# First block of a two-block network: one stream of dense products with the steps of three mixers woven in, x normed first

## The chip, the cores and the metric

The kernel runs on one core of a Trainium2 chip. The metric is device time of one execution in microseconds (us). The engines of the core are TensorE (PE in the rows; PEld is its weight load), VectorE (DVE), ScalarE (ACT), GpSimd (POOL) and SyncE (SP), which issues the DMAs.

## The reference

512 tokens of width 1024 go through a first block and then a second. All data is float32. The change is in the first block:

```
hn = rmsnorm(x, norm_g);  z = hn @ w_in          # aq ak av ag | mq mk mv mo mi mf mg | gq gk gv ga gg
y_a = band_chunk_attention(aq, ak, av, rel_bias) * silu(ag)              # 6 heads of 64
qk  = silu(causal_conv([mq, mk], conv_w))                                 # 4 taps
y_b = sigmoid(mo) * head_rmsnorm(mlstm_chunkwise(qk, mv, mi, mf)) * silu(mg)   # 6 heads of 64
y_c = head_rmsnorm(gla_chunkwise(gq, gk, gv, logsigmoid(ga @ w_alpha + b_alpha) / 16)) * silu(gg)   # 4 heads
x   = rmsnorm(x + [y_a, y_b, y_c] @ w_out, final_g)
```

The second block has a memory of 256 tokens (`mem_2`), whose keys and values (`memk`, `memv`) are made by two dense products; two layers (attention with forget gates, then multi-head latent attention, each with cross attention to the memory) and a convolutional feed-forward after each. It is not touched, except that `memk` and `memv` are computed at another time.

## The kernel before

**Engines and steps.** `schedule()` (line 2384) is one list of step names. Each engine's program runs through the whole list and, at each name, resumes its own generator for this stage (`pe_att`, `act_att`, `dve_att`, ...). So the order of work on every engine is the order of the list, and each engine's queue is in order. Semaphores tie the engines together: `q.wait_ge(*K.at(name))` waits for the event `name`. A name `barN` makes ScalarE, VectorE and GpSimd wait for all engines; it stands where memory is handed from one stage to the next.

**Stages of the first block**, in this order: `mem` (norm and products of the memory, then the norm of x and its transposes), `proj1` (dense: aq, ak, ag, av), `att`, `ya` (attention times silu(ag)), `proj2` (dense: gates, mo, mqk with convolution, mg, mv), `ml` (mLSTM, one head a step), `proj3` (dense: gg, gqk, gv, and six transposes), `gla` (gated linear attention), then `wo1` (output projection, residual, norm).

**Dense products** are float32 by three products of a high and a low part (`mm3`, lines 286 to 288). The weights come in chunks of at most 128 x 1536. A chunk n goes into the staging tile n mod 3 (DMA, line 251), ScalarE copies it to `whi` (line 269), VectorE makes `wlo` (line 278); all three have three buffers. `due` says at which step an engine splits chunk n. `pe_fm` makes a product with channels on partitions, 24 products of 512 columns; `pe_pair` makes two at a time; `pe_tm` makes one with tokens on partitions, four token tiles, in two phases with one chunk each. The results go to PSUM banks, seven of them in the ring `RA`, and are evacuated by `act_hi` (line 366 or 368) and `dve_lo` (375, 377), or `act_evac` (408) and `dve_evac` (413).

**Attention** handles items (head, tile of 128 queries), two heads at a time. At step t: scores of two items in three passes (lines 689, 692, 695), bias and maximum on VectorE (797, 800), exponential on ScalarE (762), transposes of item t-3 (710), evacuation on ScalarE (408), product with v of item t-5 (724).

**mLSTM**: per head, A (1051), scores (1058), decay on ScalarE (1083), its triangle on GpSimd (1155), product of both on VectorE (1112), output (1069); then denominators and a norm per head, `hm` scaled (1138) and multiplied by the gate into `yt` (1142).

**Gated linear attention**: levels 8, 9, 10 (tile to tile), then 0 to 6 (within a tile, by halving), then 7 (diagonal). For levels 0 to 6: a difference of `bT` on VectorE (1277), absolute value and exponential on ScalarE (1302, 1304), times k on VectorE (1279) and times q on GpSimd (1319), 16 products on 32 rows each (1339), four masked copies into `ATT` on VectorE (1394). At the end the outputs (1351, 1354).

Of the kernel before, what the change touches and what calls it, by code (L numbers as in the profile page):

```python
# [13 lines left out]
F32 = mybir.dt.float32  # L14
# [7 lines left out]
P = 128  # L22
# [113 lines left out]
class Ring:  # L136
# [10 lines left out]

    def take(self, q, name):
# [79 lines left out]


# [68 lines left out]
def pe_fm(e, q, K, key, x, kt, n, ring=None, rows=P, name=None):  # L298
# [7 lines left out]
    z.then_inc(*K.pe.up(name or key, ("wused", i)))  # L306


def pe_pair(e, q, K, keys, x, kt, n, ring=None):
# [3 lines left out]
    for k in range(kt):  # L313
        for key, (i, hi, lo), o in zip(keys, two, outs):
# [5 lines left out]
            if k == kt - 1:  # L320
                z.then_inc(*K.pe.up(key, ("wused", i)))


def pe_tm(e, q, K, key, g, x, tiles, cols, mid=None):
# [11 lines left out]
    z.then_inc(*K.pe.up(("wused", i)))  # L336
# [4 lines left out]
    for c in range(tiles):  # L341
# [5 lines left out]
        z.then_inc(*K.pe.up((key, g, "c", c), *[("wused", i)] * (c == tiles - 1)))  # L347
# [111 lines left out]
def sp_init(e, q, K):  # L459
    mem = K.d["mem_2"].rearrange("a (c p) n -> p (a c) n", p=P)  # L460
    x = K.d["x"].rearrange("a (c p) n -> p (a c) n", p=P)
    for c in range(2):
        e.dma_start(K.memt[:, c, :], mem[:, c, :]).then_inc(*K.mem_in[c].up(("mem_in", c), by=16))
    e.dma_start(K.vc[:], K.d["vecs"]).then_inc(*K.consts_in.up(by=16))
    e.dma_start(K.fb[:], K.d["fox_b_f_2"].rearrange("a n -> n a")).then_inc(*K.consts_in.up("consts", by=16))
    for _ in range(3):
        sp_load(e, q, K)
    for c in range(4):
        e.dma_start(K.xt[:, c, :], x[:, c, :]).then_inc(*K.x_in[c].up(("x_in", c), by=16))
# [6 lines left out]
def act_mem(e, q, K):  # L476
    q.wait_ge(*K.at("epsc"))
# [4 lines left out]
    q.wait_ge(*K.at("consts"))  # L482
    for kt in range(8):
        act_hi(e, q, K, ("m", "hi", kt), ("memT", kt), K.mh[:, kt, :], K.col("mem_norm", kt))
    yield
    act_token_squares(e, q, K, "x", K.xt, 4, 0, "x_in")
    q.wait_ge(*K.at(("x", "sum")))
    act_rstd(e, q, K, "x_r", K.small[:, 16:20], K.small[:, 16:20], D)
    for m in range(2):
        t = K.tmp.take(q, ("mksq", m))  # L490
        q.wait_ge(*K.at(("memk", m)))
        e.activation(t[:, 0:256], K.bank(("memk", m))[:, 0:256], ACT.Square).then_inc(*K.act.up(("mk", "sq", m)))
    yield
    for m in range(2):
        t = K.tmp.take(q, ("mkr", m))
        q.wait_ge(*K.at(("mksum", m)))
        act_rstd(e, q, K, ("mkr", m, "made"), t[:, 0:256], K.bank(("mksum", m))[:, 0:256], 64, frees=[("mksum", m)])
    yield
    act_evac(e, q, K, ("vmem", 0), ("memv", 0, "c", 0), K.vmem[:, 0, :], K.bank(("memv", 0, "c", 0))[:, 0:256])
    yield  # L500
    yield
# [5 lines left out]
def dve_mem(e, q, K):  # L507
# [5 lines left out]
    yield  # L513
    for kt in range(8):
        dve_lo(e, q, K, ("m", "lo", kt), ("memT", kt), ("m", "hi", kt), K.ml[:, kt, :], K.mh[:, kt, :],
               K.col("mem_norm", kt))
    yield
    dve_token_sums(e, q, K, "x", 4, 0)
    q.wait_ge(*K.at("x_r"))
    for c in range(4):  # L520
        e.tensor_scalar(K.yt[:, c, :], K.xt[:, c, :], K.small[:, 16 + c:17 + c], None, MUL).then_inc(*K.dve.up(("yt", c)))
    yield
    for m in range(2):
# [78 lines left out]
def dve_proj1(e, q, K):  # L602
# [7 lines left out]
    for _ in range(6):  # L610
        yield
# [2112 lines left out]
```

## Time and profile before

| | us |
|---|---|
| median of 3 runs | 1734.3 (1734.26 to 1743.34) |
| profiled execution, its time | 1752.93 |
| profiled execution, span | 1751.2 |
| mean granted TensorE clock | 0.939 of 2.4 GHz |
| end of the first block up to its output projection | 409.5 us of the span |

The page lists the busy time of each engine and, for 40 equal slices of the span (43.8 us each), the busy share in tenths and TensorE's granted clock in tenths of full speed (9 is 0.9 or more). The chain that ended last goes back from the last instruction, each piece to what released it; it shows what each moment waited for. A float32 product of the mixers has two records, so x8 in the chain is four products.

### The profile page before, as it was taken

Reading aid. Unit: us, or ns where it says so; the run is one execution under the profiler, and the core shown is the slowest. Engines: PE = TensorE matmul, PEld = TensorE weight load, DVE = VectorE, ACT = ScalarE, POOL = GpSimd, SP = SyncE. Lnnn points to the kernel's source line nnn. Section 1 sums busy time; section 2 is a strip of 40 time slices with the busy share of each in tenths; the row PEclk is TensorE's granted clock in tenths of the full one; section 3 lists DMA queues with packets and bytes.
Section 4 is the critical chain, followed back from the end, with each engine's and each line's share of the span. In section 5 each row is a group of like instructions: output and inputs, shape, how many; then the busy total and the mean of one; then the engine's idle time right before and its main releaser. Section 6 shows DMA issues by size and latency. Waiting matters only on the chain.

```text
span 1751.2 us, 20800 instructions
## 1 busy us (share of the span) xinstructions
PE 1647.5 (94%) x8398; PEld 1367.0 (78%) x8398; DVE 829.5 (47%) x1308; ACT 696.8 (40%) x1242; POOL 358.2 (20%) x285
## 2 busy tenths in 40 slices
PE   6999999949899999989999999988899899999999
PEld 6988887839678877868888888656788688888887
DVE  5332625563343466365433443337774544334442
ACT  6343432422456343344422443335553444324431
POOL 0000021320034100133401442103301244104420
PEclk9968985957899999999999999999999999999999
DMA  5401210201123100222322332111001233323331
GB/s 197 150 24 42 96 49 0 100 1 49 36 74 114 65 1 1 84 72 96 115 90 85 96 110 95 40 51 43 25 1 61 69 100 105 112 72 97 101 122 42
DMA packets 36736, 126.36 MB, mean 72 GB/s; under 512 B 4112, under 2 KB 8864, under 8 KB 36640
## 3 DMA queue, kind: packets, MB, share of 16 engines
q1 hardware_dynamic: 36640, 125.03, 22.2%
q8 instruction: 66, 1.08, 0.3%
q14 instruction: 30, 0.25, 0.0%
HBM read 122.92 MB, written 2.10 MB: 71 GB/s over the span
## 4 chain that ended last, share of the span: by engine, by line
PE 83%; DVE 8%; ACT 6%; issue 2%; DMA 1%; POOL 0%; SPq 0%; ACTq 0%; DVEq 0%
PE bank L286 22%; PE bank L287 22%; PE bank L288 22%; PE bank L724 4%; PE bank L710 2%; PE bank L1069 2%; PE bank L1058 1%; ACT tmp L762 1%; DVE tmp L1579 1%; PE bank L689 1%; DVE hlo L1583 1%; PE bank L1339 1%; ACT hhi L1571 1%; PE bank L355 1%; PE bank L1556 1%
## 5 line engine op out<-in xcount | busy, mean ns | idle before, releaser
L286 PE MATMUL bank<-hhi,whi 128*128 128x512 f32 (+1 forms) x1040 | 408.4, 393 | 3.6 <-DVE wlo L278 3.6
L287 PE MATMUL bank<-hlo,whi 128*128 128x512 f32 (+1 forms) x1040 | 406.1, 391 | 0.0
L288 PE MATMUL bank<-hhi,wlo 128*128 128x512 f32 (+1 forms) x1040 | 405.9, 390 | 0.0
L278 DVE TENSOR_TENSOR wlo<-wstage,whi 128x1024 fp32r<-128x1024 f32 (+3 forms) x206 | 279.6, 1359 | 224.9 <-ACT whi L269 218.2
L269 ACT CAST whi<-wstage 128x1024 fp32r<-128x1024 f32 (+3 forms) x206 | 229.4, 1115 | 174.3 <-PE bank L288 148.8
L1899 DVE SCALAR_TENSOR_TENSOR cr<-bank,vc,cr 128x511 f32<-128x511 f32 (+1 forms) x176 | 131.7, 749 | 225.6 <-ACT cr L1842 222.5
L286 PEld LDWEIGHTS bank<-hhi,whi 128*128 128x128 f32 (+1 forms) x1040 | 194.7, 187 | 47.8 <-DVE wlo L278 5.5
L287 PEld LDWEIGHTS bank<-hlo,whi 128*128 128x128 f32 (+1 forms) x1040 | 194.7, 187 | 42.8 <-issue 1.6
L288 PEld LDWEIGHTS bank<-hhi,wlo 128*128 128x128 f32 (+1 forms) x1040 | 194.6, 187 | 42.9 <-issue 0.8
L1842 ACT ACTIVATE cr<-bank,vc 128x512 f32<-128x512 f32 x88 | 68.5, 781 | 257.3 <-PE bank L288 254.1
L1941 POOL TENSOR_TENSOR cr<-cr,cr 128x512 f32<-128x512 f32 x44 | 91.6, 2082 | 283.3 <-DVE cr L1899 260.6
L286 PE MATMUL bank<-ahi,whi 128*128 128x512 f32 x352 | 139.5, 396 | 0.0
L288 PE MATMUL bank<-ahi,wlo 128*128 128x512 f32 x352 | 139.1, 395 | 0.0
L287 PE MATMUL bank<-alo,whi 128*128 128x512 f32 x352 | 139.0, 395 | 0.0
L286 PE MATMUL bank<-whi,hhi 128*128 128x384 f32 (+1 forms) x400 | 131.0, 328 | 0.0
L287 PE MATMUL bank<-wlo,hhi 128*128 128x384 f32 (+1 forms) x400 | 129.8, 325 | 0.0
L288 PE MATMUL bank<-whi,hlo 128*128 128x384 f32 (+1 forms) x400 | 129.6, 324 | 0.0
L1947 POOL TENSOR_TENSOR alo<-cr,ahi 128x512 fp32r<-128x512 f32 x44 | 96.8, 2201 | 120.5 <-ACT ahi L1854 120.5
L710 PE MATMUL bank<-ident,tmp 128*128 128x128 f32 x364 | 74.9, 306 | 14.3 <-ACT tmp L762 6.8
L1923 DVE TENSOR_TENSOR xT<-bank,xT 128x512 f32<-128x512 f32 x32 | 22.1, 692 | 127.4 <-PE bank L288 127.4
L286 PEld LDWEIGHTS bank<-whi,hhi 128*128 128x128 f32 x400 | 77.6, 194 | 1.6 <-issue 0.8
L288 PEld LDWEIGHTS bank<-ahi,wlo 128*128 128x128 f32 x352 | 66.0, 187 | 16.0
(358 smaller groups left out, 2390.5 us busy)
## 6 DMA issues: line engine op xcount, KB each, us to landing
wstage<-in_wts SPq DMA_DIRECT2D x148, 512.0 KB, 3.5
wstage<-in_wts SPq DMA_DIRECT2D x32, 704.0 KB, 4.0
wstage<-in_wts SPq DMA_DIRECT2D x18, 768.0 KB, 4.4
xt<-in_x SPq DMA_DIRECT2D x4, 512.0 KB, 9.3
out<-ob SPq DMA_DIRECT2D x8, 256.0 KB, 2.3
U<-in_rel_ext SPq DMA_DIRECT2D x6, 256.0 KB
wstage<-in_wts SPq DMA_DIRECT2D x3, 384.0 KB, 2.9
memt<-in_mem SPq DMA_DIRECT2D x2, 512.0 KB, 4.0
```

What stands on the lines that cost most here:

```text
L269: e.copy(K.whi[i % 3][:, 0:w], K.stage[i % 3][:, 0:w]).then_inc(*K.act.up(("whi", i)))
L278: e.tensor_tensor(K.wlo[i % 3][:, 0:w], K.stage[i % 3][:, 0:w], K.whi[i % 3][:, 0:w].bitcast(F32), SUB).then_inc(*K.dve.up(("wlo", i)))
L286: e.matmul(o, lh, rh, start=start, stop=False)
L287: e.matmul(o, lh, rl, start=False, stop=False)
L288: return e.matmul(o, ll, rh, start=False, stop=stop)
L710: z = e.transpose(b[:, j * P:(j + 1) * P], K.tmp[A.name, "P", t][:, j * P:(j + 1) * P], K.ident[:])
L724: z = e.matmul(o, A.pt[A.name, "pt", t][:, j * P:(j + 1) * P], A.heads[h].v(j), start=j == 0, stop=j == n // P - 1)
L1069: z = e.matmul(b[:, i * 65:(i + 1) * 65], scm[:, o:o + P], K.mva[:, J, h, :], start=J == 0, stop=J == i)
L1842: e.activation(t[:], K.bank(key)[:], ACT.Identity, scale=K.col(f"cw{l}", 3 * ch + 2), bias=K.col(f"cb{l}", ch)).then_inc(*K.act.up((key, " ...
L1899: e.scalar_tensor_tensor(out=t[:, s:T], in0=b[:, 0:T - s], scalar=K.col(f"cw{l}", 3 * ch + 2 - s), in1=t[:, s:T], op0=MUL, op1=ADD).then_i ...
L1941: e.tensor_tensor(g[:], g[:], v[:], MUL).then_inc(*K.pool.up(("gated", l, ch), frees=[((up, 22 + ch), "cr")]))
L1947: e.tensor_tensor(alo[:, ct, :], g[:], ahi[:, ct, :].bitcast(F32), SUB).then_inc(*K.pool.up(("alo", l, hv, ct), frees=[((up, 11 * hv + ct) ...
```

## The change

- The `mem`, `proj1`, `proj2`, `proj3` stages become one, `den`, of 48 steps. `x` (two steps) goes ahead of it: x is loaded first, normed tile by tile, transposed, split. The memory's products are steps in `den`.
- `weave` mixes steps: 34 of attention with 22 of `den` (av to mqk), 17 of mLSTM with 11 (mo to gv), 16 of gated linear attention with 11 (gv, gg, ag). The barriers `bar0` to `bar3` are gone; instead, single waits (`("att", "fin", 2)`, `("ml", "y", 5)`) guard memory that is used again.
- Banks: mixers have banks 0 to 5, dense products a ring of two (`RP`, banks 6 and 7). Attention has three banks for scores instead of four, two for transposes, one for outputs instead of two. `pe_tiles` replaces `pe_tm` in the block: one bank per token tile, both weight chunks held through all four tiles.
- A chunk is split at the first step after the last use of chunk n-3.
- SiLU and sigmoid are made of exp, ln, exp; the SiLU table isn't loaded in the block any more. For the mLSTM gate, sigmoid(mo) and silu(mg) are joined in logarithms.
- mLSTM has 20 steps (two heads and one tile column at a time) instead of 9; its gate is one multiply per head.
- Levels 0 to 6 of gated linear attention: the difference moves from VectorE to GpSimd.
- `ya` moves from VectorE to GpSimd, to the end, after `ag`.
- x is read from memory a second time for the residual (`again`), as its first tile is overwritten.
- Small tensors move within SBUF, and the scratch for descriptors is made smaller.

```diff
 def schedule():
-    out = ["init"] + ["mem"] * 7 + ["bar0"] + ["proj1"] * 15 + ["att"] * 34 + ["ya", "bar1"]
-    out += ["proj2"] * 23 + ["ml"] * 9 + ["bar2"] + ["proj3"] * 13 + ["gla"] * 16 + ["bar3"]
+    out = ["init"] + ["x"] * 2 + ["den"] * 3
+    out += weave(("att", 34), ("den", 22)) + weave(("ml", 17), ("den", 11)) + ["ml", "masks", "ml", "ml", "again", "masks"]
+    out += weave(("gla", 16), ("den", 11)) + ["den"]
     out += ["wo1"] * 23 + ["norm0", "bar4"] + ["fox"] * 25 + ["foxatt"] * 74
+def weave(*parts):
+    at = [((i + 0.5) / n, k, name) for k, (name, n) in enumerate(parts) for i in range(n)]
+    return [name for _, _, name in sorted(at)]

@@ due
-    return K.first_step[max(n - 2, 0)] - (n < 2) <= g
+    if n < 3:
+        return K.first_step[0] - (n < 2) <= g
+    return K.last_step[n - 3] < g

+def pe_tiles(e, q, K, key, g, x, tiles, cols, extra=None):
+    two = [K.chunk(q, key, g, half) for half in range(2)]
+    for c in range(tiles):
+        b = K.RP.take(q, (key, g, "c", c))
+        for k in range(8):
+            i, hi, lo = two[k // 4]
...
+            z = mm3(e, b[:, 0:cols], x.hi[:, k, c * P:(c + 1) * P], x.lo[:, k, c * P:(c + 1) * P],
+                    hi[:, k % 4, :], lo[:, k % 4, :], k == 0, k == 7)
...
+        yield

+def pe_den(e, q, K):
...
+    pe_pair(e, q, K, [("aq", 0), ("ak", 0)], x, 8, T, K.RP)
+    yield from pe_tiles(e, q, K, "av", 0, x, 4, 384)
...
+    for kt in range(6):
+        q.wait_ge(*K.at(("ya", 3) if kt < 3 else ("ml", "y", 5)))
+        pe_turn(e, q, K, ("yT", kt), lambda c: K.yt[:, c, kt * P:(kt + 1) * P], 4)

@@ act_den, mg
+        act_sigmoid_ln(e, q, K, ("mg", c), t[:, 0:384], K.bank(("mg", 0, "c", c))[:, 0:384], ("mg", 0, "c", c))
+        q.wait_ge(*K.at(("mg", "both", c)))
+        e.activation(t[:, 0:384], t[:, 0:384], ACT.Exp, scale=-1.0).then_inc(*K.act.up(("mg", "sig", c)))

@@ pool_level
     if li < 7:
+        s = 64 >> li
+        t = K.ltp.take(q, ("gl", "t", li))
...
+        e.tensor_tensor(tv, bv, bv[:, :, s - 1:s].to_broadcast([P, T // (2 * s), 2 * s]), SUB).then_inc(*K.pool.up(("gl", "d", li)))
+        q2 = K.qlp.take(q, ("gl", "q", li))
         q.wait_ge(*K.at(("gl", "e", li)))
...
+        e.tensor_tensor(q2[:], K.gq[:], t[:], MUL).then_inc(*K.pool.up(("gl", "qd", li), frees=[("gl", "t", li)]))

@@ act_gla and dve_gla, levels 8 to 10
+            q.wait_ge(*K.at(("ml", "y", 5)))
```

The order of `pe_den` is: aq 0 with ak 0; av; aq 1; ak 1; the memory's transposes (`memT`); memk 0, memk 1; memv; gate; aq 2 with the rows `frow` and `alrow`; ak 2; mv; six mqk; mo; gqk 0; mg; gqk 1; gv; gg; ag; six transposes `yT`. A product with tokens on partitions takes one step for each tile.

## Rows read from the trace of the kernel before

**Rows 1.** The page: granted clock of TensorE in 40 slices.

```profile
PEclk9968985957899999999999999999999999999999
```

**Rows 2.** Windows: length; PE, PEld, DVE, ACT, POOL busy (count); clock; DMA; GB/s.

```profile
0.00:35.00 35.00, 21.40 (x149) 20.54 (x150) 18.66 (x31) 24.14 (x56) 2.52 (x15) 0.95 0.62 232
35.00:101.00 66.00, 66.00 (x337) 60.15 (x336) 21.78 (x22) 22.05 (x28) 0.41 (x1) 1.00 0.38 123
101.00:150.00 49.00, 47.38 (x255) 41.54 (x255) 17.82 (x84) 22.85 (x72) 0.00 (x0) 0.58 0.00 1
150.00:244.00 94.00, 91.73 (x469) 80.65 (x468) 42.06 (x49) 36.30 (x48) 10.33 (x9) 1.00 0.27 87
244.00:305.00 61.00, 61.00 (x180) 41.90 (x178) 26.67 (x54) 15.11 (x41) 9.98 (x28) 0.53 0.00 1
305.00:345.00 40.00, 39.49 (x274) 37.06 (x273) 22.47 (x34) 18.39 (x32) 15.94 (x29) 0.94 0.32 109
345.00:410.00 65.00, 36.81 (x358) 33.52 (x355) 37.66 (x68) 13.85 (x31) 12.44 (x7) 0.52 0.00 1
...
600.00:700.00 100.00, 93.31 (x786) 77.90 (x784) 65.42 (x175) 41.57 (x136) 0.00 (x0) 1.00 0.02 7
```

**Rows 3.** The chain, dense products: start us, length us, what.

```profile
13.12 0.36 PE bank L316
...
35.03 0.34 PE bank L316
...
98.16 0.17 PE bank L287
...
310.18 0.12 PE bank L286
```

**Rows 4.** The chain, same positions in attention pairs and in mLSTM heads.

```profile
105.99 0.72 PE bank L689 x2
...
140.64 0.72 PE bank L689 x2
...
279.01 2.00 PE bank L1051 x2
...
290.03 2.00 PE bank L1051 x2
```

**Rows 5.** The chain in gated linear attention and the start of the output projection.

```profile
354.79 2.19 PE bank L1339 x32
...
358.39 0.64 ACT lt L1304
...
360.64 2.18 PE bank L1339 x32
...
392.25 1.47 PE bank L1351 x6
...
409.51 0.43 PE bank L286
```

**Rows 6.** Groups of instructions, 0 to 42 us: squares of x.

```profile
L394 ACT ACTIVATE tmp<-xt 128x512 f32<-128x512 f32 x8 | 4.9, 616 | 0.0
...
L394 ACT ACTIVATION_READ_ACCUMULATOR tmp<-xt 128x1 f32 x8 | 1.5, 187 | 0.0
```

**Rows 7.** Groups, 38 to 102 us: the splits of a chunk of 1536.

```profile
L278 DVE TENSOR_TENSOR wlo<-wstage,whi 128x1536 fp32r<-128x1536 f32 x5 | 8.8, 1759 | 16.6 <-ACT whi L269 16.6
L269 ACT CAST whi<-wstage 128x1536 fp32r<-128x1536 f32 x5 | 7.4, 1482 | 11.3 <-PE bank L288 11.3
```

**Rows 8.** Instructions on the tile hm: ns min/median/max, first and last start.

```profile
L1138 DVE TENSOR_TENSOR hm<-hm,small x6: 420/896/903, 281.9 to 312.7; 128x256 f32<-128x256 f32 x6
```

**Rows 9.** Groups, 345 to 410 us: the level loop.

```profile
L1394 DVE COPY_PREDICATED ATT<-msk,bank 128x512 f32<-128x512 int32 x28 | 17.8, 714 | 1.2 <-PE bank L1339 1.2
...
L1319 POOL TENSOR_TENSOR ql<-gq,lt 128x512 f32<-128x512 f32 x7 | 12.4, 1777 | 41.5 <-ACT lt L1304 41.5
...
L1279 DVE TENSOR_TENSOR kl<-gk,lt 128x512 f32<-128x512 f32 x7 | 4.8, 692 | 9.5 <-ACT lt L1304 9.5
```

More of the change, by code:

```diff
@@ L227, in chunk, with used @@
         return i, hi, lo
+    def used(self, i):
+        if self.counting:
+            self.last_step[i] = self.step
+        return "wused", i
 def half(h):
@@ L492, in act_mem @@
         e.activation(t[:, 0:256], K.bank(("memk", m))[:, 0:256], ACT.Square).then_inc(*K.act.up(("mk", "sq", m)))
+        yield
+    act_evac(e, q, K, ("vmem", 0), ("memv", 0, "c", 0), K.vmem[:, 0, :], K.bank(("memv", 0, "c", 0))[:, 0:256])
+    mk_norm(0)
     yield
[L494 to L497, printed above, removed]
+    mk_norm(1)
@@ new lines, in act_den @@
+    for i in range(6):
+        conv(MQK[i])
+        if i:
+            conv_silu(MQK[i - 1])
+        yield
+    for c in range(4):
+        b = ("mo", 0, "c", c)
+        q.wait_ge(*K.at(("memv", 0, "c", 1)))
+        q.wait_ge(*K.at(b))
+        e.activation(K.G[:, c, :], K.bank(b)[:, 0:384], ACT.Exp, scale=-1.0).then_inc(*K.act.up(("mo", "exp", c), frees=[b]))
+        q.wait_ge(*K.at(("mo", "exp", c)))
+        e.activation(K.G[:, c, :], K.G[:, c, :], ACT.Ln, bias=1.0).then_inc(*K.act.up(("mo", "ln", c)))
+        if c == 0:
+            conv_silu(MQK[5])
+        yield
@@ new lines, in act_den @@
+    q.wait_ge(*K.at(("att", "fin", 2)))
+    q.wait_ge(*K.at(("gqk", 0)))
+    e.activation(K.gq[:], K.bank(("gqk", 0))[:], ACT.Identity, scale=32 ** -0.5).then_inc(*K.act.up("gq", frees=[("gqk", 0)]))
+    yield
+    for c in range(4):
+        t = K.tmp.take(q, ("mg", c))
+        act_sigmoid_ln(e, q, K, ("mg", c), t[:, 0:384], K.bank(("mg", 0, "c", c))[:, 0:384], ("mg", 0, "c", c))
+        q.wait_ge(*K.at(("mg", "both", c)))
+        e.activation(t[:, 0:384], t[:, 0:384], ACT.Exp, scale=-1.0).then_inc(*K.act.up(("mg", "sig", c)))
+        yield
@@ L566, in pe_proj1 @@
[L566 to L582 removed]
+    akk(2)
@@ L683, in score @@
     def score(ts):
-        at = [(t, A.items[t][1], A.heads[A.items[t][0]], A.n(t), K.RS.take(q, (A.name, "S", t))) for t in ts]
+        at = [(t, A.items[t][1], A.heads[A.items[t][0]], A.n(t), A.S.take(q, (A.name, "S", t))) for t in ts]
         z = {}
@@ L1328, in pe_gla @@
             k2, q2 = K.kl["gl", "k", li], K.ql["gl", "q", li]
-        banks = [K.RA.take(q, ("gl", "B", li, h)) for h in range(4)]
+        banks = [K.RG.take(q, ("gl", "B", li, h)) for h in range(4)]
         rows = [slice(32 * h, 32 * h + 32) for h in range(4)]
@@ L2402, with run @@
 SCHEDULE = schedule()
-def run(e, q, K, signal, stages, ahead=None):
+def run(e, q, K, signal, stages, ahead=None, behind=None):
     begun = {}
@@ L2514, in pairs, with above @@
         return Ring(K, [Buffer(K, tuple(sb(f"{name}{p}{i}", shape, F32R, scope) for p in "hl"), after) for i in range(n)])
+    @contextmanager
+    def above(n):
+        with ExitStack() as scope:
+            if n:
+                sb(f"below{next(count)}", [P, n // 4], scope=scope)
+            yield scope
+    count = itertools.count()
     banks = [Buffer(K, ctx.enter_context(nc.psum_tensor(f"bank{i}", [P, 512], F32))) for i in range(8)]
@@ L2566, in memory @@
-    with ExitStack() as s:
-        K.fgr = sb("fgr", [P, D], scope=s)
-    first.close()
+    with above(35328) as s:
+        K.dts, K.scs, K.hm = ring("dt", 3, [P, T], s), ring("scm", 4, [P, 1280], s), sb("hm", [P, 4, 6, 64], scope=s)
+        K.kl, K.ql, K.lt = ring("kl", 2, [P, T], s), ring("ql", 2, [P, T], s), ring("lt", 2, [P, T], s)
+        K.qlp, K.ltp = (Ring(K, r.buffers[::-1], r.place) for r in (K.ql, K.lt))
+        K.gq, K.gk, K.gv = sb("gq", [P, T], scope=s), sb("gk", [P, T], scope=s), sb("gv", [P, 4, 256], scope=s)
+        K.msk = sb("msk", [P, 7, P], scope=s)
```

1027 lines of the change are left out of this document (531 added, 496 removed).

## The prediction

> **What bounds the kernel now.** Start with the granted-clock line of the page [rows 1]: the second half of the run is at full clock, the first ten slices are not. The windows by stage [rows 2] say which part of the first block that is. It ends at 409.5 us, where the first product of its output projection stands in the chain [rows 5]. Its dense stages (35 to 101, 150 to 244, 305 to 345) have TensorE busy for nearly all their time at a clock of 0.94 to 1.00. Between them stand three mixers, 49, 61 and 65 us long at 0.58, 0.53 and 0.52, so at the lower level, 1.2 GHz. In attention and mLSTM TensorE is busy all the time: they are TensorE work done at half speed. In gated linear attention it is busy 36.8 of 65 us, and the chain [rows 5] shows a loop from TensorE to the masked copy, the decay on ScalarE and back, 5.85 us a level. So the block loses in two ways: work at 1.2 GHz, and waits.
>
> **TensorE's work, at full clock.** The change removes no product. Spacings in the chain [rows 3] are 0.17 us for 384 columns and 0.12 for 256; 35.03 to 101 us holds 144 products of 512 and 192 of 384, which gives 0.227 with 0.174. The block has 360, 480 and 288 of these: 82 + 83.5 + 34.5 = 200 us. Transposes and small products: about 6 us (56 at 0.11, an estimate: 128 columns, near the 0.12 of 256). Attention: two pairs of heads lie between 105.99 and 140.64 at half clock [rows 4], 17.3 us each, so 8.7 at full clock and 26 for three. mLSTM: 11.0 us a head at half clock [rows 4], 5.5 at full, 33 for six. Gated linear attention: eight levels of 2.18 us, three small ones, and the output from 392.25 to 409.5 [rows 5]; halved, 8.7 + 1.3 + 8.6 = 18.6. Sum 284 us.
>
> **Start.** x goes first now, memory is moved into the stream (its products are in the 200). Before, the first memory product stood at 13.12 us [rows 3], after two tiles of 128 tokens; x has four. Each adds two squares, (0.616 + 0.187) x 2 = 1.6 us [rows 6], and, because the root is now taken tile by tile, a sum and a root, 0.6 to 0.8 (an estimate: four small operations of about the 0.187 that the accumulator's read takes): 13.1 + 4.3 to 4.8 = 17.4 to 17.9. I take 17.4. The x stream began at 35.03, so this gives 17.6 us, less the memory work that goes elsewhere. If nothing ever stalled, the block would end at 17.4 + 284 = 301 instead of 409.5: a saving of 108. That is the outer bound; the rest of this part is what is lost of it.
>
> **Weight chunks: 4.5 us at one place, some more later.** `pe_tiles` asks for both halves of its weights before its first product, and there are three buffers. The second chunk of `av` takes the buffer of `aq` 0, free only when the opening pair ends; then come two evacuations on ScalarE (2 x 0.6, an estimate from the 0.64 of an activation on 512 columns [rows 5]), the copy 1.48 and the subtraction 1.76 [rows 7]: 4.5 us of idle TensorE. gv to gg and gg to ag have the same shape, but with steps of the level loop between; they fall into idle time counted below. memk to memv: 1 us.
>
> **Attention woven with dense (22 steps).** Dense: 264 x 0.227 + 144 x 0.174 + 96 x 0.12 + 3 for transposes and rows = 99.5; with attention's 26, 125.5 us. In the windows before that hold this work and more (35 to 244) VectorE is busy 81.7 us and ScalarE 81.2 [rows 2]; with the activations that are added, 90 of 125: neither is the bound. But queues are in order and a dense result is evacuated before the next softmax: where two attention steps stand side by side (12 of 34) and the second scores, TensorE runs into it, 0 to 2 us each; I take 6 in all. The memory transposes take four turns of a ring with two banks (3 us), the memory sums 1, and the two gate rows take the bank that `aq` 2 has just filled (2 us). Lost: 12, between 5 and 25.
>
> **mLSTM woven (11 steps).** Dense: 192 x 0.174 + 48 x 0.227 + 24 x 0.12 = 47; with mLSTM's 33, 80 us. Each gate step `mg` makes VectorE wait for ScalarE (two activations, add, activation, multiply on 384 columns; at most 0.64 each as at 512 [rows 5], I take 2.8 us) with mLSTM's products queued behind; six places where mLSTM steps adjoin, 1 us each: 6, between 2 and 15.
>
> **mLSTM to gated linear attention: a new wait.** The level-8 evacuations now wait for the last mLSTM output, because their tiles lie over mLSTM's. VectorE has, after `gqk` 1: the preparation of levels 8 and 9 (about 5 us with ScalarE's exponentials between), the last two heads' denominators and sums (3), then 12 multiplies. The six `hm` ones take 0.42 to 0.90 us [rows 8], as they meet GpSimd or not; with 0.7 and 0.45 they are 7 us. 15.5 us in all, of which TensorE fills 7 (last outputs, gv, level 8): 8.5 lost, between 3 and 12.
>
> **The level loop moves to GpSimd.** Now each level has, in order on GpSimd, the difference, the wait for ScalarE's two activations (0.64 each [rows 5]) and the q multiply. The trace has the q multiply at 1.78 us against 0.69 for the k multiply on VectorE [rows 9]; I price the difference the same: 1.78 + 1.27 + 1.78 + 0.1 = 4.95 us a level, seven levels 35 us, and 1.8 for clearing ATT and 2 for two gain multiplies ahead: 38.5 us from the last mLSTM output to the last level. TensorE has 25 us for that stretch (6 dense steps of 2.9, levels 7.4): 13.8 idle. Of a difference on GpSimd no row exists; from a free one (0.69 as on VectorE, hidden) to 2.5 us, the idle time is 7 to 19. The Trainium skill (GPSIMD Engine Reference, 4.1 Engine selection) puts two-input elementwise work on VectorE and calls GpSimd some 2 times slower, which speaks against this move; the trace is harsher, 1.78/0.69 = 2.6. By the page a level would be about 4.2 us and the loss 8.5 instead of 13.8. VectorE's copies, four of 0.714 a level [rows 9], and a k multiply are 3.55 us, below 4.95, so it isn't the bound. The other stage, `ag` and the outputs, 27.5 us of TensorE, stands behind the loop.
>
> **Tail.** `ya` is now made last: three activations, two multiplies, one of them on GpSimd, then transposes and the split ahead of the output projection: 3.7 + 1.8 = 5.5 us that lay under gated linear attention before. In return the projection starts at full clock: its first products lasted 0.43 us each [rows 5] against 0.17; for some 2.6 us that is 1.3 us.
>
> **Clock.** The pattern of the trace: the clock fell at attention's start, where the window's only idle time is (1.6 of 49 us [rows 2]), and stayed down although TensorE was busy after that; in mLSTM it fell while TensorE was fully busy, with products on 64 rows and fewer; dense products brought it back (0.94 on average from 305 to 345, so at most 5 us at the lower level); the later attention, 600 to 700, keeps 1.00 with 93% busy and no dense step. Woven, dense steps of 2.9 to 5.4 us stand between pieces of other work of at most some 5 us, so I expect 1.00 in the first two weaves with short dips and less sure in the third: 5 us, between 0 and 20.
>
> **Costed at nothing.** Six table loads go, SiLU becomes exp, ln, exp: 22 activations become 62, at 0.4 to 0.64 some 20 us more on ScalarE in 350, which has the slack above; six reciprocals go from VectorE. x is loaded a second time under the third weave, more than 30 us before its use; were it late, 2 MB at the 232 GB/s of the first window [rows 2] is 9 us. The new rule for splitting chunks moves each at most to the step after the last use; ahead of later stages it can only come earlier: 0, between -3 and 3 us.
>
> **Sum.** Idle: 4.5 + 1 + 12 + 6 + 8.5 + 13.8 + 5.5, and 5 of clock = 56. 301 + 56 = 357 against 409.5, and 1.3 after it: -54 us. The profiled execution (span 1751.2, its own time 1752.9) is 1% above the median of the runs, 1734.3; the terms are absolute times, so I take 54 from the median as well: 1680.
>
> **Rivals.**
> - The stream packs better than I count: GpSimd's difference costs little, queues meet nowhere, idle 10 to 25 us. Fox attention, 93% busy with the same queue structure [rows 2], speaks for it; the transition wait and the GpSimd order, which are in the code, against. Saves 85 to 100: about 1642. Chance 0.17.
> - The third weave stays at 1.2 GHz: TensorE is 65% busy there, as in the gated stage before (57% at 0.52). Then its 52 us of work take up to 104, part of it in idle time that was there anyway: 20 to 30 us more, a saving of some 28, 1706. Chance 0.12.
> - On the other side: the clock does not come back in any weave, since half of each is work of the kinds at which it fell. The price is as many microseconds as there is work at half speed. It decides from 54 us on, a fifth of the 284; if all three weaves were cold (125 + 80 + 50), they would cost 255 and the kernel take 1935. That the clock was back at full within 5 us of dense products at 305 [rows 2] speaks against it. Chance 0.06.
> - It does little: in-order waits of a round trip at each of the 80 woven steps, 0.6 us more each, eat it all; within 9 us of before. The later attention with 74 steps shows no such waits. Chance 0.05.
>
> **Numbers.** My forecast 0.60. Its own range: idle from 4 + 1 + 5 + 2 + 3 + 7 + 4 + 0 = 26 to 4.5 + 1 + 25 + 15 + 12 + 19 + 6 + 20 = 102 if all ends met, 1650 to 1726; the ends do not all meet, and half way to each is 1665 to 1703. With the first two rivals at its sides the 8 in 10 range is 1640 to 1710. 0.5% (9 us) is about what a measurement of this kernel can tell. Faster 0.89, within 0.5% 0.05, slower 0.06.
>
> **What would show it.** The output projection's first product near 355 us of the span (right: 340 to 370). x's first dense product at 17 to 18. A gap of 4 us ahead of `av`. Clock 1.00 in 60 to 260. GpSimd's level pair at 4.9 us apart, and TensorE waiting for it; TensorE idle before level 9. After the block all stages as long as before. Wrong would be: half clock over more than 40 us of the weaves; VectorE busy above 80% there; a stage after the block changed by over 5 us.

## The result: 1.9% slower, not 3% faster

The kernel after takes 1771.2 us in the median, beside 1735.5 for the kernel before in the same session: ratio 1.0190, 95% interval 1.0145 to 1.0234. The forecast was 1680. The profiled execution after took 1773.65 us (span 1771.9). One execution of four, at 2343.62 us and a clock of 0.639, is left out of the ratio. The profiled execution of before took 1752.93 us, longer than any of the four that its median is made of (1734.3 to 1743.3), so the two traces differ by only 20.7 us where the medians differ by 36.

The page of the kernel after, first the clock line that answers to [rows 1]:

```profile
PEclk8889988989999969999999999998899999999999
```

The deep dips of before (slices 3, 7, 9 and 10) are gone, and the block is never long at full clock either. Two dips are new, one around slice 15 (1.2 GHz from 615.4 to 653.0 us) and one at slices 28 and 29, in stages that the change does not touch. Where the block ends, TensorE's rows show (start, length, count, idle before and its releaser):

```profile
411.26 4.18 PE L385 MATMUL bank<-ident,xT 128*128 128x128 f32 x24 [3.43 <-POOL xT L943]
416.03 0.41 PE L299 MATMUL bank<-whi,hhi 128*128 128x384 f32 x1 [0.59 <-DVE hlo L405]
```

The output projection begins at 416.03 us, 6.5 later than before [rows 5], where 357 was forecast. The windows by stage of the kernel after (columns as in [rows 2]); the first five are the block (start; attention weave; mLSTM weave; level loop; tail):

```profile
0.00:47.00 47.00, 27.55 (x122) 23.83 (x123) 17.82 (x25) 20.17 (x41) 2.93 (x16) 0.89 0.61 213
47.00:212.00 165.00, 145.83 (x797) 122.64 (x795) 71.88 (x158) 71.29 (x150) 0.14 (x1) 0.91 0.19 61
212.00:312.00 100.00, 84.91 (x410) 69.05 (x411) 33.45 (x65) 37.12 (x78) 21.60 (x50) 0.86 0.13 43
312.00:373.00 61.00, 40.42 (x452) 36.60 (x451) 36.44 (x72) 23.02 (x48) 25.53 (x18) 0.89 0.22 83
373.00:416.00 43.00, 33.21 (x232) 32.46 (x232) 21.25 (x35) 18.00 (x34) 4.85 (x6) 0.88 0.15 49
...
600.00:610.00 10.00, 10.00 (x60) 10.00 (x59) 1.78 (x2) 2.02 (x3) 0.00 (x0) 1.00 0.15 52
610.00:620.00 10.00, 6.35 (x30) 3.97 (x29) 5.44 (x12) 4.22 (x13) 0.00 (x0) 0.77 0.15 53
620.00:650.00 30.00, 30.00 (x144) 25.18 (x145) 13.20 (x41) 8.30 (x29) 0.00 (x0) 0.50 0.00 1
650.00:660.00 10.00, 9.44 (x77) 7.65 (x73) 6.30 (x14) 4.29 (x13) 0.00 (x0) 0.85 0.01 2
660.00:700.00 40.00, 38.24 (x337) 32.01 (x337) 26.23 (x70) 16.95 (x55) 0.00 (x0) 1.00 0.01 1
```

Read each window for two losses: its length less PE's busy time is idle, and (1 less the clock) times its length is what the lower clock takes. The two overlap: a low clock costs nothing while TensorE idles. In the gated stage before, 28.2 of 65 us were idle at 0.52, so some 13 of that row's 31 us of clock are idle time already. With the granted clock laid beside TensorE's gaps, of 84 us of clock in the block before 13 lie over idle time, of 46 in the kernel after 8. The table counts only the clock over busy time:

| block, us | length | idle | clock, TensorE busy | rest: work at full clock |
|---|---|---|---|---|
| before [rows 2] | 410 | 46 | 71 | 292 |
| forecast | 357 | 68 | 5 | 284 |
| after | 416 | 84 | 38 | 294 |

The forecast's 68 holds its whole start of 17.4 us, in which TensorE has 6 us of transposes; its 284 compares with 288 behind the first dense product. So the work was counted rightly to 4 us, and the change did take 33 us of clock loss away. It put 38 us of idle time in their place, where 22 had been forecast.

The clock's loss lies where the waits are. After its first transposes TensorE waits 13 times for 3 us or more in the block, and each time a stretch at 1.2 GHz begins during the wait or within 1 us of its end: behind the wait that ends at 73.3 it is 72.7 to 86.4, behind those that end at 246.8 and 302.9 it is 246.8 to 253.6 and 301.4 to 308.2. Of the other three such stretches one begins in a wait of 1.8 us; two (from 127.3 and from 260.5) begin where no wait of 1 us stands.

The second finding is outside: 620 to 650 us runs at 1.2 GHz, where before stayed at 1.00 from 600 to 700 [rows 2]. From the output projection to the end it is 1355.9 us (1771.9 - 416.0) against 1341.7 (1751.2 - 409.5). That understates this loss, as e1 shows.

Who TensorE waits for in the attention weave (47 to 212 us; total, times, longest):

```profile
PE bank L1040 <- DVE att_mx L1148: 13.0, 4, 4.2
PE bank L299 <- DVE acol L870: 1.8, 1, 1.8
PE bank L1040 <- DVE akl L405: 1.5, 1, 1.5
```

in the mLSTM weave (212 to 312 us):

```profile
PE bank L1259 <- DVE scm L1314: 9.6, 3, 4.3
PE bank L1272 <- DVE hm L1327: 5.5, 1, 5.5
```

and in the level loop (323 to 380 us):

```profile
PE bank L1437 <- DVE ATT L1494: 15.9, 4, 6.4
PE bank L1434 <- DVE AX L443: 5.2, 1, 5.2
PE bank L1437 <- DVE AX L443: 2.6, 1, 2.6
```

Three queues show how such a wait comes about. At 73 us (kernel after, timeline of all engines, load of weights left out):

```profile
70.51 1.05 ACT L282 CAST whi<-wstage 128x1024 fp32r<-128x1024 f32 x1
70.64 0.69 DVE L405 TENSOR_TENSOR akl<-bank,akh 128x512 fp32r<-128x512 f32 x1 [1.03 <-ACT akh L396]
71.59 1.23 DVE L291 TENSOR_TENSOR wlo<-wstage,whi 128x1024 fp32r<-128x1024 f32 x1 [0.26 <-ACT whi L282]
72.73 0.42 DVE L1148 CUSTOM_DVE_ANT_0 att_s<-bank,U 128x256 f32<-128x256 f32 x1
...
73.31 0.69 PE L1040 MATMUL bank<-akh,aqh 64*128 64x384 f32 x2 [4.16 <-DVE att_mx L1148]
...
346.83 0.72 POOL L936 TENSOR_TENSOR gg<-gg,ggn 128x256 f32<-128x256 f32 x1 [1.74 <-DVE gg L900]
347.63 1.04 POOL L1413 TENSOR_TENSOR lt<-bT 128x512 f32<-128x512 f32 x1
...
349.36 0.63 ACT L1396 ACTIVATE lt<-lt 128x512 f32<-128x512 f32 x1
350.10 0.69 DVE L1371 TENSOR_TENSOR kl<-gk,lt 128x512 f32<-128x512 f32 x1 [3.35 <-ACT lt L1396]
350.12 1.79 POOL L1418 TENSOR_TENSOR ql<-gq,lt 128x512 f32<-128x512 f32 x1 [1.46 <-ACT lt L1396]
350.70 2.56 DVE L1494 COPY_PREDICATED ATT<-msk,bank 128x512 f32<-128x512 int32 x4
...
352.30 2.09 PE L1437 MATMUL bank<-ql,kl 32*128 32x128 f32 x32 [5.82 <-DVE ATT L1494]
...
611.64 1.23 DVE L291 TENSOR_TENSOR wlo<-wstage,whi 128x1024 fp32r<-128x1024 f32 x1 [0.57 <-ACT whi L282]
612.78 0.48 DVE L1810 TENSOR_SCALAR kmg<-kmn,vc 128x512 f32<-128x512 f32 x1
...
613.41 1.14 PE L1040 MATMUL bank<-kmg,mqT 64*128 64x256 f32 x8 [2.94 <-DVE kmg L1810]
```

First place: TensorE's next scores need the bank that the maximum at 72.73 frees; on VectorE the split of `ak` and a chunk's split, 1.9 us of work for the dense stream, stand ahead of it. Second, 346 to 351 us: GpSimd first makes a gate multiply that waits for the dense step, then the difference; ScalarE follows; VectorE waits for ScalarE with the k multiply at the head of its queue, and the four masked copies, whose operands are long there, lie behind it; TensorE waits 5.82 us. The longest waits for `scm` (4.3 us) and for `ATT` (6.4) have more ahead of them: from 242.4 and from 374.0 us VectorE splits two chunks of 1536, 3.43 us, before it makes what TensorE waits for. Third, 611 us, outside the block: a chunk split that the new rule put there stands ahead of `kmg`, which opens the forgetting attention.

### The profile page after: what moved, and what is told of

The parts are those of the page before. It is cut to its first block, busy times and chain, and to the rows that moved or that the text cites. A ratio compares the mean times of both kernels' runs of the same rounds, so it can differ in the third digit from the quotient of the medians.

```text
span 1771.9 us, 20805 instructions
## 1 busy us (share of the span) xinstructions
PE 1627.9 (92%) x8398; PEld 1352.7 (76%) x8398; DVE 821.4 (46%) x1321; ACT 713.8 (40%) x1282; POOL 364.1 (21%) x286
## 4 chain that ended last, share of the span: by engine, by line
PE 79%; DVE 10%; ACT 8%; POOL 2%; issue 2%; DMA 0%; POOLq 0%; ACTq 0%; DVEq 0%
PE bank L299 21%; PE bank L300 21%; PE bank L301 21%; PE bank L1075 4%; PE bank L1061 2%; DVE wlo L291 2%; PE bank L1040 2%; ACT whi L282 2%; DVE tmp L1675 1%; ACT tmp L1113 1%; DVE hlo L1679 1%; PE bank L1272 1%; PE bank L1652 1%; ACT hhi L1667 1%; PE bank L332 1%
## 5 line engine op out<-in xcount | busy, mean ns | idle before, releaser
L300 PEld LDWEIGHTS bank<-hlo,whi 128*128 128x128 f32 (+1 forms) x1040 | 195.9, 188 | 42.3 <-issue 1.0
L299 PEld LDWEIGHTS bank<-ahi,whi 128*128 128x128 f32 x352 | 66.1, 188 | 16.7 <-issue 3.3
L1061 PE MATMUL bank<-ident,tmp 128*128 128x128 f32 x304 | 63.4, 309 | 15.9 <-ACT tmp L1113 12.1
```

Source lines behind the costliest of these rows:

```text
L299: e.matmul(o, lh, rh, start=start, stop=False)
L300: e.matmul(o, lh, rl, start=False, stop=False)
L1061: z = e.transpose(b[:, j * P:(j + 1) * P], A.P[A.name, "P", t][:, j * P:(j + 1) * P], K.ident[:])
```

## The experiments

Ratios are to the kernel before, run beside each group on the same chip; its median was 1743.5 beside e1 to e4, 1742.0 beside e5 to e8, 1734.7 beside e9 to e12 and 1743.4 beside e13 and e14. So across groups compare ratios, not medians; the kernel after, 1.0190 (1.0145 to 1.0234), ran in none of them. "Projection" is the start of the output projection's first product in the profiled execution. Spans are of single profiled executions; the kernel after has 1771.9 and 416.0.

| run | median us | ratio, 95% interval | span | projection |
|---|---|---|---|---|
| e1 old rule past the block | 1747.0 | 1.0031 (1.0014 to 1.0048) | 1743.4 | 416.0 |
| e2 new rule in before | 1770.9 | 1.0142 (1.0082 to 1.0202) | 1770.5 | 403.1 |
| e3 aligned | 1766.7 | 1.0145 (1.0111 to 1.0178) | 1762.7 | 406.6 |
| e4 serial | 1786.6 | 1.0267 (1.0229 to 1.0306) | 1783.2 | 425.5 |
| e5 banks | 1772.8 | 1.0167 (1.0109 to 1.0224) | 1771.2 | 415.4 |
| e6 difference on VectorE | 1771.7 | 1.0162 (1.0109 to 1.0214) | 1772.6 | 416.7 |
| e7 level order | 1764.3 | 1.0114 (1.0062 to 1.0165) | 1756.0 | 408.0 |
| e8 splits behind | 1745.1 | 1.0025 (0.9992 to 1.0059) | 1743.5 | 398.5 |
| e9 = e1+e3+e5+e7 | 1718.2 | 0.9909 (0.9895 to 0.9924) | 1716.5 | 390.5 |
| e10 = e9, e8 in the block | 1710.3 | 0.9855 (0.9831 to 0.9879) | 1708.8 | 378.3 |
| e11 = e10 without e3 | 1710.4 | 0.9867 (0.9852 to 0.9882) | 1709.3 | 383.4 |
| e12 = e10, tail order | 1705.1 | 0.9834 (0.9816 to 0.9853) | 1703.8 | 377.6 |
| e13 = e12, serial | 1750.6 | 1.0050 (1.0011 to 1.0088) | 1746.1 | 421.7 |
| e14 = e12 without e5 | 1708.9 | 0.9803 (0.9754 to 0.9852) | 1705.1 | 378.9 |

**e1, the split rule outside the block.**

```
 def due(K, n, g):
     if n < 3:
         return K.first_step[0] - (n < 2) <= g
+    if K.first_step[n - 2] >= SCHEDULE.index("wo1"):
+        return K.first_step[n - 2] <= g
     return K.last_step[n - 3] < g
```

> The kernel after, but from the first output projection on a chunk is split by the old rule (as soon as the chunk two before it is first used), not by the new one (once the buffer's last user has been issued). The first block is untouched. Theory A: outside the block the loss is the new rule's. It puts one more chunk split (ScalarE 1.06 us, VectorE 1.23 us) ahead of the head of the forgetting attention and ahead of latent attention; TensorE then idles 2.94 us at 613.41 where it idled 1.14 before, and 4.40 us near 1210 where it idled 2.83, and runs at 1.2 GHz from about 616 to 653 where it had stayed at full clock. By this 15 us come back at the first place and 6 at the second: about 1750 (1745 to 1755) against 1771, with a granted clock of 1.00 from 600 to 700. Rival: the clock falls there by chance, or because the first block leaves another state, and the splits are hidden: no change, 1766 to 1776, and the clock still falls at 616.

Theory A, with a median inside its range; the projection stays at 416.0, and the span falls by 28.5 us where 21 had been expected. The windows of e1:

```profile
610.00:620.00 10.00, 7.99 (x56) 5.93 (x55) 5.62 (x15) 4.39 (x16) 0.00 (x0) 1.00 0.00 1
620.00:650.00 30.00, 29.22 (x252) 23.92 (x251) 21.05 (x62) 13.93 (x49) 0.00 (x0) 1.00 0.01 1
```

The wait for `kmg` is 1.14 us instead of 2.94, and 620 to 650 stays at full clock; VectorE does 21 us of softmax there instead of 13. That is 15.4 us up to the first feed-forward (its first convolution starts 360.5 us after the projection instead of 375.9), the other 13.1 lie behind it. Most of these are clock too: from the first feed-forward on it takes 17.1 us in the kernel after and 8.7 in e1; in latent attention after is at 1.2 GHz from 1206 to 1216 and from 1240 to 1250 us, e1, whose work there stands some 17 to 25 us earlier, only from 1190 to 1197. With the same split rule e1 is also 14.3 us shorter behind the projection than the profiled execution of before (1327.4 against 1341.7), all of it behind the first feed-forward's start; no run asks why.

**e2, the same rule put into the kernel before**: `due` with the new rule for chunks of the output projection and later, and loads issued behind a step's own instructions.

> The converse: the kernel before, with the new split rule from the first output projection on (and the loads issued behind a step's own instructions on the load queue, as the kernel after has them, without which the order does not close). Its first block is untouched. Theory A: it loses what the kernel after loses outside the block: a gap of about 3 us at the head of the forgetting attention (near 607 us), 1.2 GHz for some 35 us after it, and a smaller loss at latent attention: +15 to +25 us, 1750 to 1760 against 1735. Rival: the rule costs nothing, as the prediction had it: within 3 us of 1735.

The converse holds: +1.4%, at the upper end, though one of its four executions took 1751.6 us and the others 1770.6 to 1772.2. Windows of e2:

```profile
600.00:610.00 10.00, 6.40 (x30) 4.32 (x30) 5.34 (x12) 4.17 (x13) 0.00 (x0) 0.74 0.18 53
610.00:640.00 30.00, 30.00 (x147) 25.01 (x145) 13.69 (x42) 8.28 (x29) 0.00 (x0) 0.50 0.00 1
```

The same wait, 2.94 us, and the same half clock behind it. From the projection on it is 1367.4 us against 1341.7. (Its first block, which is before's own work, ended at 403.1 instead of 409.5: attention from 101 to 150 us had a clock of 0.83 in this execution and 0.58 in [rows 2]. So the block before is 403 to 410 us long.)

**e3, attention's steps in pairs.**

```
-    out += weave(("att", 34), ("den", 22)) + weave(...
+    for name in weave(("att", 17), ("den", 22)):
+        out += [name] * (2 if name == "att" else 1)
+    out += weave(...
```

> The kernel after, with one line of the schedule changed: attention's 34 steps are woven in as 17 pairs, each pair beginning with the step that scores, with a dense step between pairs. In the kernel after the four long waits of scores (4.16, 1.56, 3.83 and 3.49 us) stand where two steps adjoin and the second scores, because on VectorE the softmax that frees the bank is then queued behind a dense step's split. Theory A: those waits go. With their idle time alone that is 13 us: 1758. Theory B, A and the clock: each wait is followed by 4 to 8 us at half clock or near it, and that goes as well: 20 to 25 us, 1746 to 1751, the granted clock above 0.95 from 60 to 200. Rival: the wait only moves to another place of the pair (two scores now follow one dense step): within 4 us of 1771.

The four waits for `att_mx` are gone, and others, up to 4.2 us, came. The attention weave ends at 199.5 instead of 211.9 us: 7 us less idle time (12.2 instead of 19.2) and, over busy time, 7 us less lost by the clock (0.96 instead of 0.91). So both theories see their part there, but 3 us are given back in the level loop, and by the span 9.2 us arrive, less than the 13 of theory A alone. In the ratios, whose intervals overlap, it can't be told from the kernel after.

**e4, nothing woven.**

```
-    out += weave(("att", 34), ("den", 22)) + weave(("ml", 17), ("den", 11)) + ["ml", "masks", ...
+    out += ["den"] * 22 + ["att"] * 34 + ["den"] * 11 + ["ml"] * 17 + ["ml", "masks", ...
-    out += weave(("gla", 16), ("den", 11)) + ["den"]
+    out += ["den"] * 11 + ["gla"] * 16 + ["den"]
```

> The kernel after with nothing woven: the same steps, the dense ones of each third in one piece (22, 11, 11) and attention, mLSTM and gated linear attention behind them each in one piece; x first, the level loop on GpSimd, the tail and the split rule stay. It asks what weaving alone brings. Worked out from the traces: start 21.5, dense products and small ones 206, gaps 4 + 3, attention 49, mLSTM 61 and gated linear attention 65 as long as they were alone, tail 8: the output projection begins at about 418 us, against 416 in the kernel after: 1773 in all. Theory A: what weaving saves in clock it gives back in queue waits, so 1765 to 1780. Rival 1: the weave is a net gain of some 30 us or more as predicted, and the loss is elsewhere (start, level loop, tail, rule): 1800 or above. Rival 2: the weave is a net loss by itself: below 1755.

Between theory A and rival 1: 0.8% above the kernel after, with intervals that just overlap, 11 us in the span and 9.5 at the projection. Weaving is worth only that in this kernel. Attention alone took 40 us, at a mean clock of 0.87, not the 49 of [rows 2], mLSTM 55 at 0.57, gated linear attention with the tail 73 at 0.56.

**e5, the banks of x's transposes.** Before the first dense product, k tiles 0 and 1 take banks 6 and 7, not tiles 6 and 7.

> The kernel after, but the transposes of x for k tiles 0 and 1, not 6 and 7, take the two banks of the ring that the dense stream uses. In the kernel after the first dense product waits until 21.52 us for the last two splits of x (6.92 us idle), because they free its banks. Theory: it starts about 4 us earlier, at 17.5, and all that follows with it: 1767 against 1771. Rival: the stream then runs into the splits of the later k tiles, or into the gap ahead of av: within 1 us of after.

TensorE's row of e5:

```profile
17.52 0.76 PE L329 MATMUL bank<-hhi,whi 128*128 128x512 f32 x1 [3.00 <-ACT hhi L398]
```

and the row of after to set beside it:

```profile
21.52 0.76 PE L329 MATMUL bank<-hhi,whi 128*128 128x512 f32 x1 [6.92 <-DVE hlo L407]
```

So the start can be where it was forecast, at 17.5, and the whole gains nothing that can be told: the lead is 4.0 us at the first product, 2.2 where mLSTM's weave begins (209.7 against 211.9), 0.7 at the projection. With equal waits, single dense steps took 1.5 us more here: the one at 146.5 us 6.12 us instead of 4.61, the one at 225.2 5.92 instead of 4.39. The clock lies differently over the same work: behind the wait that ends at 143.6 (147.6 in the kernel after) it is low for 6.8 us instead of 3.4, and from 225.7 for 3.4 us where after has no such stretch. (The expectation of e14 below puts the lead at 209 us at 4.3 us; it was 2.2.)

**e6, the level's difference back on VectorE** (the line moved from `pool_level` to `dve_level`, ahead of the wait for the exponentials).

> The kernel after with the difference of each level back on VectorE, ahead of the exponentials' wait, as before. Theory P (the prediction's): GpSimd is the bound of the level loop, so without the difference, measured 1.05 us there, a level gets 1 us shorter: -7 us, 1764. Theory Q: the loop is bound by the order of the queues (VectorE waits for ScalarE's exponentials ahead of the masked copies, ScalarE and GpSimd wait for gate work of the dense stream), and VectorE, which now also has the difference between two waits, gets no better: within 3 us of 1771, or up to 7 slower.

Theory Q: no change that can be told. Taking the difference off GpSimd gains nothing, so GpSimd alone was not what bounded the loop, although a q multiply takes 1.79 us there. The difference takes 0.76 us on VectorE here, so this run can't tell a loop bound by the order from one bound by both engines; e7 can.

**e7, the order within the level loop.**

```
 def dve_gla:
-        if at_i + 2 < len(LEVELS):
+        if at_i == 0:
             dve_level(e, q, K, LEVELS[at_i + 2])
         for h in range(4):
             ... copy_predicated ...
+        if 0 < at_i and at_i + 2 < len(LEVELS):
+            dve_level(e, q, K, LEVELS[at_i + 2])
 def pool_level: difference of li + 1, then q multiply of li
```

> The kernel after with two changes of order in the level loop and no change of work: GpSimd makes the difference of the next level ahead of the q multiply of this one, and VectorE makes the four masked copies of a level ahead of the k multiply of the level two on, which waits for the exponentials. In the kernel after TensorE idles 19.7 us in six waits between 330 and 380 us, the longest 5.82 and 6.42. Theory Q (the order of the queues is what costs): the long ones go, a level's GpSimd time is 1.05 + 1.80 without the 1.46 that it waits for ScalarE: -10 to -14 us, 1757 to 1761, the output projection at 402 to 406. Rival: the loop is bound by VectorE's copies and the round trip through TensorE, -3 us or less.

By the order, then, if less than expected. The waits for `ATT` fall from 15.9 to 8.8 us in total, and the projection comes 8.0 us earlier, short of the 10 to 14 expected: one of 6.4 us, where VectorE and ScalarE split two weight chunks ahead of the copies, stays. In the ratios the intervals of e7 and the kernel after still overlap. 7.9 us more came outside the block, and that is the clock. `kmg` was waited for as long as in the kernel after, yet these are the windows of e7:

```profile
600.00:610.00 10.00, 6.78 (x35) 5.33 (x35) 3.77 (x8) 2.95 (x8) 0.00 (x0) 0.84 0.26 83
610.00:620.00 10.00, 10.00 (x65) 7.49 (x66) 6.34 (x18) 4.67 (x18) 0.00 (x0) 0.82 0.01 2
620.00:650.00 30.00, 28.65 (x250) 23.80 (x249) 21.69 (x61) 14.05 (x47) 0.00 (x0) 1.00 0.00 1
```

**e8, splits behind a step's own work.** `act_split` and `dve_split` run ahead of a step only for a chunk that is used within two steps, and behind it for all that are due:

```
+def pressing(K, n, g):
+    return n < len(K.order) and K.first_step[n] <= g + 2
...
-    while due(K, K.nlo, g):
+    while due(K, K.nlo, g) and (all or pressing(K, K.nlo, g)):
```

> The kernel after, but a chunk's split that is not needed by the next two steps is issued behind a step's own work on ScalarE and VectorE instead of ahead of it; everywhere in the kernel. Theory: queued splits ahead of the softmax and of mLSTM's decay are what TensorE waits for in the first two weaves (four waits of scores, 13 us; three waits of scm, 9.6 us) and at the head of the forgetting attention (15 us with the clock). If most of it goes: 1735 to 1750. Rival A: the waits only change places, as chunks then come later, with gaps on VectorE's wlo instead: 1765 to 1775. Rival B: only the place outside the block answers: about 1755.

Within the range: the block is 17.5 us shorter, the rest 10.9. Waits in its mLSTM weave, 209 to 297 us:

```profile
PE bank L1264 <- DVE scm L1319: 5.5, 3, 3.5
PE bank L1277 <- DVE hm L1332: 2.5, 2, 2.1
```

8.0 us instead of 15.1; the weave is 12 us shorter (209.1 to 297 against 211.9 to 312). In the attention weave one of the four waits of scores went (3.83), one fell from 4.16 to 3.12 and one grew from 3.49 to 5.78, and a wait for `ml` grew from 1.0 to 3.3: 18.5 us idle instead of 19.2, so there rival A holds. At the forgetting attention the wait was 1.1 us and the clock stayed at 1.00.

**e9 to e12, together.**

> The kernel after with four of the edits at once: the old split rule from the output projection on, attention's steps aligned in pairs, the two banks freed first, the order in the level loop. Alone they gave about -27, -8, 0 and -8 to -15 us (the last with a clock dip that happened to be short outside the block). If they add up without the doubtful parts: 27 + 9 + 0 to 4 + 8 = 44 to 48: 1725 to 1730, below the kernel before (1735 to 1742). Rival: they share one cause (the clock after a long wait), so that together they bring little more than the best alone: 1740 or above.

> The four edits together, and in the first block alone a split that is not needed by the next two steps goes behind a step's own work. Alone and everywhere, that order gave -30 us: the output projection at 398.5 instead of 416.0, the rest 11 shorter. Theory: with attention aligned it still takes the mLSTM waits (4.32, 3.47 and 5.45 became 0.8, 3.5 and 2.1) and the clock with them, 8 to 12 us: 1715 to 1722, the projection at 380 to 388. Rival: aligned attention and splits behind take the same waits, so within 4 us of the four together.

> The kernel of e10 with attention's steps woven as in the kernel after, not in pairs. It asks whether aligning the steps and putting the splits behind are two cures or one. If one: equal to e10 within 3 us. If two: 4 to 8 us slower than e10, with waits of scores of 3 us and more (near 70 and 140 us) still there.

> The kernel of e10, with the last transposes of the block and their splits in another order: the k tiles 3 to 5, which hold mLSTM's output and are ready long before, ahead of 0 to 2, which wait for GpSimd's last multiply of the attention output (3.43 us idle, with 8.2 us from the last ag product to the output projection). Theory: 1 to 2 us less than e10, as only the transposes and three splits move under the wait. Rival: the wait stays the last thing and the gain is below what can be told, 0 to 1 us.

e9 beats the kernel before, by 0.9%, and by more than the sum: 55.4 us of span beside the kernel after, where 45 had been expected. e10 takes another 0.5%, 8 us, at the lower edge of its 8 to 12, although its projection comes 12.2 us earlier. e12 ends at 0.9834: 1.7% faster than before and 3.5% faster than the change as made, with the same work. e11 has the waits of scores back (3.1 and 5.8 us) and its projection 5.1 us later, but in the total it can't be told from e10. The tail's order in e12 brought 0.7 us at the projection; what its total has beyond that came elsewhere, and the intervals of e10 and e12 overlap. The block of e12 in one window:

```profile
0.00:378.00 378.00, 322.49 (x2010) 276.25 (x2011) 183.22 (x354) 167.00 (x349) 50.65 (x91) 0.92 0.24 83
```

Idle 55.5 us, and 25 lost by the clock over busy time, from 84 and 38 in the kernel after.

**e13 and e14, what was open.**

> The kernel of e12 with nothing woven (attention's pairs then have no meaning). Theory A: what weaving brings is hidden in the kernel after by the waits that it makes; without them it is worth far more than the 14 us (0.8%) between e4 and the kernel after. From the traces: dense at full clock, attention 40 us (26 at full clock), mLSTM 55 (33), gated linear attention 50 at least with the new order (29 with its dense steps taken out): 40 to 55 us slower than e12, 1745 to 1760. Theory B: weaving is worth its 14 us and no more, the edits help both alike: 1715 to 1722.

> The kernel of e12 without the two banks freed first. Alone that edit brought nothing, although the first dense product came 4.0 us earlier and the lead was still 4.3 us at 209 us; between 225 and 239 the clock took most of it back. Theory: the lead is real and the clock's part is a matter of where the waits fall, so here, with shorter waits, it may be kept: 3 to 5 us slower than e12. Rival: a lead at the start is always lost to a later wait: within 1 us.

Theory A for e13: weaving is worth 44.1 us at the projection, 42.3 in the span and 2.2% in the ratios, three to nearly five times what e4 and the kernel after show. The mixers alone in e13 (attention, mLSTM, gated linear attention):

```profile
160.00:209.00 49.00, 39.97 (x252) 34.06 (x251) 23.09 (x89) 27.77 (x78) 0.00 (x0) 0.72 0.13 44
258.00:311.00 53.00, 48.65 (x181) 33.57 (x181) 18.29 (x47) 18.09 (x47) 14.37 (x46) 0.59 0.08 26
361.00:416.00 55.00, 36.28 (x362) 32.98 (x359) 35.23 (x60) 16.48 (x35) 18.56 (x16) 0.55 0.03 10
```

e14 starts 4 us later than e12 (21.4 against 17.5) and is 1.3 us behind at the projection; the ratios overlap. So the rival is nearer, and whether the total keeps a microsecond of it stays open.

## Why the prediction was wrong

Right: TensorE's work (284 us forecast, 288 left behind the first dense product when idle and clock are taken off), the gap ahead of `av` (4.5 forecast, 3.9 measured), a wait at the transition (8.5, was 5.2), about 4 us idle in the tail (5.5), the loads of x and SiLU's extra activations at nothing, and that weaving pays, once the queues allow it: 44 us.

Of the 91 us between the 1680 forecast and the 1771 measured, 59 lie ahead of the output projection (416.0 instead of 357), 15.5 behind it, and some 17 are the base: the forecast took off the median, 1734.3, what it had counted in an execution of 1752.9. The 59 are, to 1 us, 33 of clock, 17 of idle time behind the start, 4 of the start and 4 of work.

Wrong, by size:

1. **Clock, "5 us, between 0 and 20": 46 us, 38 of them while TensorE was busy.** This step failed most: 33 of the 59 us. The forecast reasoned from what kind of work runs at which clock, and from the later attention [rows 2], which stays at 1.00 at 93% busy with waits under 1.2 us. The weave has waits of 3 to 6 us, and in the kernel after each of 13 such waits has its low stretch. Where such waits go, so does clock loss: in the attention weave of e3 and in the mLSTM weave of e8 (15.1 us idle became 8.0, and 13.7 us of clock 6.8). The number 5 would have had to be worked out with the waits: two terms of the sum were treated as independent. The forecast's own sign of being wrong, half clock over more than 40 us of the weaves, came true with 82 us from 47 to 416.
2. **Queue waits in the first two weaves, 12 and 6: 19 and 15 us.** The place was named rightly (two attention steps side by side, the second scoring), the price "0 to 2 us each", 6 in all, was 13.0 for four waits: it left out that a chunk's split (1.23 us on VectorE, behind 1.05 on ScalarE) is queued there too. e3 and e8, which change only order, take 7 us of idle time away each, e3 in the first weave and e8 in the second.
3. **The level loop, 13.8: 21.2 us** (26.4 idle from 312 to 379, less the 5.2 of the transition), and for another reason. GpSimd's difference took 1.05 us, not 1.78, which would have made the forecast's 4.95 us a level 4.2; e6 shows that taking it off GpSimd gains nothing, e7 that the order is worth 8.0 us. The difference on GpSimd takes 1.5 times the 0.69 us that it took on VectorE before, the q multiply 2.6 times the k multiply. The Trainium skill (GPSIMD Engine Reference, 4.1 Engine selection) has one figure for both, about 2; the measurements decide, and they lie on either side of it.
4. **Start, 17.4: 21.5 us.** The forecast overlooked that the stream's two banks were last held by x's k tiles 6 and 7. e5 shows the mechanism; at the projection the 4 us are worth 0.7 in e5 and 1.3 between e14 and e12.
5. **"The new rule for splitting chunks: 0, between -3 and 3": 28.5 us in the span of e1, 1.6% in the ratios.** "It can only come earlier" was true, and was the fault: earlier means ahead of something else in an in-order queue. e1 and e2 show it from both sides. The other sign came true here: a stage after the block changed by over 5 us. Without this the change as made is within 0.3% of before, by e1, which is still no gain.

Beside the forecast's rivals: "it does little, for in-order waits eat it" came nearest, with 0.05; none had the clock follow from the waits, and none had a cost outside the block. That the waits bring the low clock is shown by their place and by the edits that remove them; why two low stretches of the block, and those of the kernel before at attention and mLSTM, begin without a wait of 1 us was not tested.

## What to carry to other kernels

- When two streams are woven on in-order engines, list for every freed bank what stands ahead of it on the engine that frees it, the background work (weight splits) too. The order within a step decided between 1.9% slower and 1.7% faster here, with no instruction added.
- An idle stretch of 3 us on TensorE can cost 15 us behind it (e1), or 3 (e7). Price waits and clock together, and look for new waits in the stages that the change leaves alone.
- A rule that moves background work "earlier" is not free: check what it now precedes at the head of each later stage.

## What the runs showed of the hardware

- The same wait of 2.94 us for `kmg` stands in e2 to e7 and in the kernel after. In six of these seven traces (starts of `kmg` from 603 to 624 us) the clock was at 1.2 GHz for 37 to 41 us behind it, although TensorE was busy for nearly all of that (30 of 30 us from 620 to 650 in the kernel after); in e7 for about 7 us only ((1 - 0.84) x 10 + (1 - 0.82) x 10 = 3.4 us lost, at half speed). With a wait of 1.1 us at this place (before, e1, e8 to e14) it never fell there. So a wait of that length has no one price.
- Because of this a gain ahead of such places can vanish (4.0 us in e5) or double (8.0 in the block of e7, 15.9 in its span), and single traces carry some 5 us of it. Attention alone, the same code, ran at 0.58 and at 0.83 in two executions of before's block.
- GpSimd's difference with a broadcast operand took 1.05 us on 128x512, its multiply of two full tiles 1.79.
